# Two transformer stacks in fp32 on one core: the turned middle tile's place in the experts' steps

## What is computed

```python
def moe_ffn(x, w_router, router_bias, w_gate, w_up, w_down):
    ...
    h = jax.nn.silu(jnp.einsum('nd,edf->enf', xt, w_gate)) * jnp.einsum('nd,edf->enf', xt, w_up)
    h = h * gates.T.astype(h.dtype)[:, :, None]
    y = jnp.einsum('enf,efd->nd', h, w_down)
    return y.reshape(B, S, D)
```

## Time and profile before

| | us |
|---|---|
| median of 3 runs | 3812.29 |
| lowest, highest of them | 3807.23, 8128.77 |
| profiled execution, its own time | 3800.46 |
| its span, first to last instruction | 3798.7 |
| TensorE busy in the span | 3430.3 (90%) |
| VectorE, ScalarE, GpSimd busy | 2028.5, 1448.2, 290.2 |
| mean granted TensorE clock | 0.898 of full |

### The profile page before, as it was taken

The page is one execution under the profiler, slowest core; times in us unless marked ns, Lnnn a source line. Parts: engine busy times, 40 slices in busy tenths (PEclk is TensorE's granted clock), DMA queues, the critical chain, the costliest instruction groups (busy, mean ns, idle before and its releaser), DMA issues.

```text
span 3798.7 us, 42690 instructions
## 1 busy us (share of the span) xinstructions
PE 3430.3 (90%) x14478; PEld 2641.8 (70%) x14478; DVE 2028.5 (53%) x3448; ACT 1448.2 (38%) x2224; POOL 290.2 (8%) x203
## 2 busy tenths in 40 slices
PE   8889788888987988799997899989999889879998
PEld 6546666666556766578875688867887667658886
DVE  4783576646855676554537553546343543455343
ACT  4543466635433566422222322233222444432221
POOL 0001022210001122200000100010000000010000
PEclk9767799989567999899998899989999889889998
DMA  3101199712001699222321222323223211012232
GB/s 120 37 1 42 37 307 314 265 40 69 1 1 58 219 318 303 77 86 94 94 94 36 67 97 94 99 73 127 94 94 120 96 39 62 28 34 94 96 99 76
DMA packets 174977, 389.48 MB, mean 103 GB/s; under 512 B 11313, under 2 KB 70065, under 8 KB 174193
## 3 DMA queue, kind: packets, MB, share of 16 engines
q1 hardware_dynamic: 173424, 377.45, 30.2%
q0 software_dynamic: 1408, 10.23, 0.8%
HBM read 381.34 MB, written 6.29 MB: 102 GB/s over the span
## 4 chain that ended last, share of the span: by engine, by line
PE 70%; DVE 13%; DMA 7%; ACT 4%; DVEq 3%; issue 2%; SPq 0%; POOL 0%; ACTq 0%; POOLq 0%
PE ps L507 18%; PE ps L509 18%; PE ps L508 17%; DMA gate_up_stage<-in_w_gu 7%; PE ps L584 4%; PE ps L600 4%; DVE moe_lo L1478 4%; PE ps L590 2%; ACT moe_hi L903 2%; PE ps L655 1%; PE ps L724 1%; PE ps L557 1%; DVE tmp L1688 1%; DVE xs_lo L1676 1%; PE ps L574 1%
## 5 line engine op out<-in xcount | busy, mean ns | idle before, releaser
L1224 DVE TENSOR_TENSOR w_lo<-w_stage,w_hi 128x1024 fp32r<-128x1024 f32 (+3 forms) x360 | 461.8, 1283 | 956.0 <-ACT w_hi L903 953.1
L507 PE MATMUL ps<-xs_hi,w_hi 128*128 128x512 f32 (+1 forms) x2032 | 825.0, 406 | 109.8 <-DVE xs_lo L1676 75.2
L509 PE MATMUL ps<-xs_hi,w_lo 128*128 128x512 f32 (+1 forms) x2032 | 813.4, 400 | 0.0
L508 PE MATMUL ps<-xs_lo,w_hi 128*128 128x512 f32 (+1 forms) x2032 | 813.1, 400 | 0.0
L903 ACT ACTIVATE w_hi<-w_stage 128x1024 fp32r<-128x1024 f32 (+3 forms) x360 | 393.3, 1092 | 1038.1 <-PE ps L509 1024.5
L507 PEld LDWEIGHTS ps<-xs_hi,w_hi 128*128 128x128 f32 (+1 forms) x2032 | 389.2, 192 | 227.7 <-issue 74.3
L509 PEld LDWEIGHTS ps<-xs_hi,w_lo 128*128 128x128 f32 (+1 forms) x2032 | 390.1, 192 | 90.6
L508 PEld LDWEIGHTS ps<-xs_lo,w_hi 128*128 128x128 f32 (+1 forms) x2032 | 391.4, 193 | 85.3
L1478 DVE TENSOR_TENSOR moe_lo<-gate_up_stage,moe_hi 128x1024 fp32r<-128x1024 f32 x224 | 277.9, 1281 | 137.4 <-ACT moe_hi L903 137.1
L507 PE MATMUL ps<-h_hi,w_hi 128*128 128x512 f32 x704 | 276.8, 393 | 0.0
L509 PE MATMUL ps<-h_hi,w_lo 128*128 128x512 f32 x704 | 276.5, 393 | 0.0
(11 more groups left out here) (322 smaller groups left out, 4925.5 us busy)
## 6 DMA issues: line engine op xcount, KB each, us to landing
gate_up_stage<-in_w_gu SPq DMA_DIRECT2D x112, 1024.0 KB, 6.1
w_stage<-in_f_gu SPq DMA_DIRECT2D x174, 512.0 KB, 3.5
down_stage<-in_w_dn SPq DMA_DIRECT2D x112, 512.0 KB, 5.4
w_stage<-in_f_dn SPq DMA_DIRECT2D x64, 704.0 KB, 4.1
w_stage<-in_w_in SPq DMA_DIRECT2D x28, 512.0 KB, 3.4
w_stage<-in_d_qk SPq DMA_DIRECT2D x24, 512.0 KB, 3.5
w_stage<-in_w_out SPq DMA_DIRECT2D x16, 512.0 KB, 3.5
w_stage<-in_d_v SPq DMA_DIRECT2D x12, 512.0 KB, 3.5
```

The source lines that it names most:

```text
L507: pe.matmul(o, lh, rh, start=start, stop=False)
L508: pe.matmul(o, lh, rl_, start=False, stop=False)
L509: return pe.matmul(o, ll, rh, start=False, stop=stop)
L1224: tt(w_lo[:, s, 0:n], stage[:, s, 0:n], w_hi[:, s, 0:n].bitcast(F32), ALU.subtract).then_inc(w_split, 1)
```

## The change

The turned tile's instructions go to another place in three lists. On TensorE the turn of step st follows one weight unit of step st+1 in place of two. On ScalarE and VectorE the high and the low half of the turned tile of step st go ahead of units 0 and 1 of step st+2.

```diff
@@ TensorE, moe
                 for st in range(STEPS):
-                    for u in range(2):
-                        if st + 1 < STEPS:
-                            gate_up(st + 1, u)
+                    if st + 1 < STEPS:
+                        gate_up(st + 1, 0)
                     turn_h(st)
-                    for u in (2, 3):
+                    for u in (1, 2, 3):
                         if st + 1 < STEPS:
                             gate_up(st + 1, u)
                     down(st)
@@ ScalarE, moe
                 for st in range(STEPS):
+                    act.wait_ge(ht_full, st0 + st + 1)
+                    copy(ht_hi[:, st % 2, :], ps[:, 2 + st % 2, 0:256]).then_inc(ht_hi_done, 1)
                     if st + 2 < STEPS:
                         hi(st + 2, 0)
                         hi(st + 2, 1)
-                    act.wait_ge(ht_full, st0 + st + 1)
-                    copy(ht_hi[:, st % 2, :], ps[:, 2 + st % 2, 0:256]).then_inc(ht_hi_done, 1)
@@ VectorE, experts
                 for st in range(STEPS):
+                    v.wait_ge(ht_hi_done, st0 + st + 1)
+                    tt(ht_lo[:, st % 2, :], ps[:, 2 + st % 2, 0:256], ht_hi[:, st % 2, :].bitcast(F32), ALU.subtract)\
+                        .then_inc(ht_split, 1)
                     if st + 2 < STEPS:
                         lo(st + 2, 0)
                         lo(st + 2, 1)
-                    v.wait_ge(ht_hi_done, st0 + st + 1)
-                    tt(ht_lo[:, st % 2, :], ps[:, 2 + st % 2, 0:256], ht_hi[:, st % 2, :].bitcast(F32), ALU.subtract)\
-                        .then_inc(ht_split, 1)
```

## The result

The changed kernel takes 3783.32 us in the median of 5 runs (3778.5 to 3787.66), the kernel before 3807.23 beside it: ratio 0.9936, 95% interval 0.9921 to 0.9952. That is 24 us less and far inside 2%, so "within 2%", and inside my range. The profiled execution took 3783.32 us, its span is 3781.6; against the profiled execution of before (3800.46, span 3798.7) it won 17.1 us, which happens to be the sum that I gave (16.6). The forecast of 3795 us is 12 us above the median. It was built on 3812.29 for the kernel before, which took 3807.23 beside the changed one: 5 of the 12 us. The other 7 are the change itself, 24 us by the medians where I gave 17.

The account below looks back on a forecast made before the run. The experts' loop of gate/up half 0 transfer, ScalarE's moe_hi and VectorE's moe_lo bounds the kernel. Terms 6.7 + 3.4 + 2.5 + 4 = 16.6 us, taken as 17 off 3812.3, give 3795 us; range 3764 to 3822.

Parts of the forecast that it names:

- What bounds the kernel: Experts' steps: the loop of half 0 transfer, moe_hi, moe_lo and next transfer fills 10.26 us; TensorE needs 8.7.
- The waits move, they are not won: TensorE's 54.6 us of down-matmul waits for h_turned_lo fall under 10; as much appears at the turn for h_slot.
- Term (a): Experts' moe_lo pairs on VectorE: 6.7 of 10.0 us excess goes, as GpSimd's subtraction ends before any due moe_lo.
- T: Zero point for times in an experts' step: gate/up half 0 has landed and its moe_hi begins (572.33 in the step shown).
- Term (b): Nine experts' steps before the tails, where the chain detours through half-rate down matmuls on TensorE: 9 x 0.38 = 3.4 us.
- Term (c): Last experts' steps, no transfer left: unit 5 starts earlier, 0.8 us in layer 0, 1.7 in layer 1, 2.5 together.
- Term (d): Down transfers issued 0.4 to 1.2 us earlier, half 1 0.3: half 0 lands earlier, 4 us, bounds 0 to 53.
- The same loop: Sign of being right: the experts' chain stays the loop over gate/up half 0, with no down matmuls in it.
- Period 9.95 us: Sync queue in the experts' steps: the period of the gate/up issues goes from 10.26 to some 9.95 us.
- rival C: ScalarE's wait for the turn, now ahead of units 0 and 1, enters the loop: slower, 3822 us; chance 0.11.
- Rival A: Queue empties, every half 0 transfer takes 5.1 us; DMA floor 9.5 us a step, 3765 us; chance 0.10.
- Rival B: Transfers are the bound and give everything back, half 0 waits longer; only the tails' gain stays: 3810 us, chance 0.22.

Follow-up runs that it names:

- TensorE's order alone: Kernel before with only TensorE's list reordered (turn after one unit), ScalarE's and VectorE's lists as before: 3802.15 us, ratio 0.9991.
- The moved tables: Changed kernel with the selection tables' instruction (sel_t) moved behind the splits of units 0 and 1: 3778.69 us, ratio 0.9934.
- the short subtraction: GpSimd's subtraction cut to 32 of 1024 columns from each layer's second step: on the kernel before 3764.68 us (0.9880), on the changed kernel 3754.58 us (0.9856).
- The second down buffer: Second stage buffer for the second down transfer: on the kernel before 3770.17 us (0.9908), on the changed kernel 3758.40 us (0.9880).
- ScalarE's and VectorE's order alone: Changed kernel with TensorE's list put back (turn after two units), ScalarE's and VectorE's lists in the new order: 3777.54 us, ratio 0.9938.
- the turn after three units: Changed kernel with TensorE's turn after three units of the next step, not one: 3783.79 us, ratio 0.9955.
- the last kernel: Changed kernel with a gate/up transfer for each unit, the selection tables moved and a second buffer for the second down transfer: 3726.23 us, ratio 0.9794.

## Why the prediction was right, and where it wasn't

**What bounds the kernel.** Right. Transfers end last before and after; halving their bytes wins 55 us from the changed kernel, and giving TensorE its tile earlier wins nothing (TensorE's order alone, 0.9991).

**The waits move, they are not won.** Right. For the matmuls `h_turned_lo` went from 54.6 to 4.0 us and `h_slot` from 1.4 to 46.5. I had said "as much": 45 came for 51 that went.

**Term (a), the excess of the `moe_lo` pairs, 6.7 us.** The pairs are at 2.36 to 2.37 throughout, as forecast. What I missed stands one instruction further on. I worked out GpSimd's new start (about T+7) and its end (up to T+9.9) and asked only whether a `moe_lo` is due in that time, though I had `sel_t` and its 2.63 us at worst in front of me. The traces have it from T+7.2 to T+10.1 in the median. `sel_t` is due just then, and in most of its 14 times it was held for 2.1 us. The moved tables show that this cost little here: the chain lost these detours and took up transfers. One reading under (a) was off: in the step shown, half 0 landed 8.7 us after T (583.39 to 592.05) and not 9.3, which is the distance of the issues.

The Trainium skill, "SBUF — State Buffer", section "SBUF: two separate sides", says that whichever of the two starts first keeps the shared port for its whole instruction, a VectorE instruction with two SBUF inputs or in a two-port mode on the one side. The rows agree in both directions: GpSimd's subtraction at 2.84 us in the median behind unit 4's `moe_lo` (2.40 before), and `sel_t` at 2.62 us behind GpSimd (0.48 with the short subtraction).

**Term (b), the nine detours over TensorE, 3.4 us.** Right in kind, too clean in my check. I expected no down matmuls in the chain. Five detours are left, at half rate among them, and they reach ScalarE over the turn and the down matmuls, since the turn is what TensorE is now late for.

**Term (c), the tails, 2.5 us.** Mis-sized: 6.2 us. The direction and the place were right.

**Term (d), the transfers, 4 us out of 0 to 53.** This term was sized too small. I took its value by the mean transfer and took back half for a fuller queue, and I treated "issued 0.4 to 1.2 us earlier" as a small thing. The second down buffer shows that of the release times that I tested on the kernel before, the issue of the second down transfer is worth most: 34 us hang on it. The change brings that issue forward in passing (6.37 us behind half 0 in place of 7.10), because unit 5's `moe_hi` hardly waits for TensorE any more (12.3 us in all for `moe_hi`, 75.7 before).

How much (d) was, three estimates from these runs say. With the buffer in both kernels the change is worth some 11 us, and 24 less 11 is 13. The half 0 transfers (the last 25 steps of each layer) took 6.20 us in the mean before and 5.98 after: 0.22 us over 48 steps is 11. With the buffer in both kernels that gain is absent, 5.46 and 5.57 us. And the 17.2 us of the steady steps less the 10.1 of (a) and (b) as I gave them leave 7. So (d) was some 7 to 13 us and not 4, and no run fixes it closer. The near hit of the sum in the profiled execution is then partly luck: 23.6 us won in the experts against 16.6 forecast, and 6.5 given back in parts that I had not looked at.

**"The same loop".** Wrong. The loop has the same instructions, but over half 1: 39 of 39 where it was none of 43. `h_turned_lo` used to stand between units 1 and 2 and so in half 1's way; what I did not ask is which of two like loops is the tighter when both gain. ScalarE's and VectorE's order alone does it (44 of 44 half 1), TensorE's doesn't (36 of 37 half 0). The two loops are close: with the tables moved 35 of 46 are half 1, with the turn after three units 34 of 45. That half 1 ends last because it is queued behind half 0 is my reading; no run took that apart.

**The other checks.** Period 9.95 us forecast, 9.90 measured. GpSimd's start at about T+7 forecast, T+7.2 measured. DMA share 0.95 forecast; 0.90 to 1.00 in seven stretches of 50 us. The waits of ScalarE for the turn (rival C) are there with 15.6 us, and with 41.6 us in the kernel with the turn after three units, whose ratio of 0.9955 can't be told from 0.9936: C's mechanism is real, and the 27 us that I gave it did not come. Rival A (short transfers throughout) did not come, 14 of 39 are short. Rival B (everything given back) didn't either. What it says of long transfers after short steps still shows here and there: 9.31 us is the longest of the changed kernel, right after one of 5.19.

Still open: why the rest of the program gives 6.5 us back, and why four transfers of 0.5 MB move more bytes in a microsecond than two of 1 MB. They are issued earlier and their pieces are half as long, and no run took the two apart.

## What to carry to other kernels

When the bound is a loop of transfers, list for each transfer of the step what releases its issue and how far ahead of the critical one it stands. A small transfer that is released late can delay the large one behind it. Here that was worth 34 us, more than the whole change, while the most visible wait of TensorE (54.6 us) only changed its place. A wait that moves from one place of an engine's queue to another was worth nothing here; what the reordering did to the release times of buffers was. And when an instruction of GpSimd moves, look up everything that VectorE has due in its new place, not only what it collided with in the old one.

## What the runs showed of the hardware

**Transfers in one queue.** The time of a 1 MB gate/up transfer went with what was issued shortly before it. In the chain of the kernel before, 28 half 0 transfers were issued 2 to 3 us after the second down transfer: 6.69 us in the mean, 7 of them short (under 5.7). The 13 issued later than 3 us after it took 5.73, 8 short. All half 0 transfers of the changed kernel divide alike: 23 with 6.81 us and 27 with 5.28. With the second down buffer in the kernel before, all but one lie over 4 us after it, and 5.52 is the mean. It is no fixed law of the distance: with the short subtraction, at 4.14 us in the median, only 13 of 27 are short.

**Small transfers can win.** Four transfers of 0.5 MB a step reached 349 to 352 GB/s in the stretches where two of 1 MB had 314 and 318 (345 in their best of seven), and with the tables moved and the second buffer 346 to 371 in seven stretches. The DMA share in such stretches reads 1.02 to 1.08. It is a sum over the packets' times; a share that can pass 1 doesn't tell how full the queue is, and 0.93 was no sign of a full one. The floor of 9.5 us a step that I built on it for rival A doesn't exist: the last kernel issues 95 unit transfers in 210.2 us, from 479.78 to 690.01, so 8.85 us a step, with all its bytes.

**A held instruction pays for its whole neighbour.** `sel_t` costs 0.48 us alone and 2.62 behind GpSimd's 2.4 us; it moves between these two values with the place of an instruction on another engine.
